# Differential attention, head by head: another order for VectorE's rotation products, combinations and output additions, and TensorE's next scores placed between sample products and value products

## The chip, the cores and the metric

The program runs on one core of a Trainium2 chip. The metric is the device time of one execution in microseconds. Three runs of the kernel before took 3537.03, 3538.32 and 3538.99 us (median 3538.32). The profile shows one execution of its own, which took 3538.83 us around a span of 3537.0 us from the first to the last instruction.

## The reference, cut to what matters

The reference is one step of a two-layer decoder over 1024 prompt tokens and 8 sample tokens (each of the 8 has 256 past positions in a paged cache). Layer 0 is a Mamba-2 mixer and an MLP. Layer 1 is differential attention with 8 heads, and an MLP. The change lies in the attention alone, which for one head computes

```python
sc = jnp.einsum('bqhmd,bkhmd->bhmqk', qi, k) * scale     # m = 0, 1: two score maps of width 64
sc = jnp.where(kpos[None, :] <= qpos[:, None], sc, -jnp.inf)
p = jax.nn.softmax(sc, axis=-1)
w = p[:, :, 0] - lam * p[:, :, 1]                         # the combination
o = jnp.einsum('bhqk,bkhe->bqhe', w, v)                   # values of width 128
o = rms_norm(o, subln_g) * (1.0 - lam_init)
out += o @ w_o[rows of this head]
# q and k come from projections of x, rotated: x1*cos - x2*sin, x2*cos + x1*sin
```

The eight sample tokens do the same against their past keys and values and their own new ones.

## The kernel before

The activations stand transposed in SBUF, 128 features by 1032 tokens a tile. The weights come as a stream of units of 128x1024 numbers. For each unit GpSimd makes a high and a low part (`split`, L321: the high part is L326, the low part L329), and a product is three matmuls: high by high, high by low, low by high. GpSimd starts on a unit when its load is there and when TensorE has begun the unit that frees the slot (`unit_begun`).

The attention stage works head by head. Each engine has its own hand-written order of the work of head n, a function `attend` (TensorE L724, ScalarE L1140, VectorE L1668), and runs its instructions strictly in that order; semaphores tie the engines together. Head 0 is written out, heads 1 to 6 are a loop, head 7 is written out. In head n three kinds of work are woven together:

- The queries of head n are taken in eight blocks, step i = 0 to 7, of growing width 128(i+1). TensorE computes both score maps into four PSUM banks (`scores`, L596, with the causal mask added by two small matmuls, L613). VectorE takes the row maxima (`maxima`, L1581), ScalarE the exponentials with their sums (`scores_exp`, L1060). VectorE weights and subtracts (`combine`, L1588: a reciprocal, a 128x1 operation L1593, a wide operation L1595, then `w_ready`). TensorE transposes the result (`turn`, L616), ScalarE copies it (`turned`, L1072), TensorE multiplies by the values (`values`, L630), ScalarE takes the result out (`output`, L1078). `scores(i)` may start when the exponentials of step i-1 have been taken (`p_ready`).
- The sample tokens: `sample_rows`, `sample_weights` and `sample_values` on TensorE (L695 to L720), and on VectorE `sample_max` (a copy out of PSUM, L1617, and a maximum, L1619), `sample_shares`, `sample_spread` (L1627) and `sample_out` (L1634). Together with `values` they share one PSUM bank, whose turns are counted by `m_free`.
- What belongs to the neighbouring heads. If `ahead`, TensorE projects queries, keys and values of head n+1 (`fill`, L638, three chunks for each; the matmuls are L647), and VectorE rotates them: two products over 128x1032 (`rope_products`, L1570) and their sum. If `fin`, head n-1 is normalized and multiplied by its rows of the output weights (`out_jobs`, L681: j = 0 to 7, three chunks each, into three banks; matmuls L690). VectorE adds every chunk to the residual (`add_outputs`, L1656), which frees its bank (`u_free`). Two of these three banks are also banks of the scores, so `scores(4)` waits for all 24 additions.

The line numbers are those of the profile.

Of the kernel before, what the change touches and what calls it, by code (L numbers as in the profile page):

```python
# [94 lines left out]
def half_of(m):  # L95

    return slice(HD * m, HD * m + HD)
# [23 lines left out]
def program(nc, a, o):  # L121
    with ExitStack() as ctx:
# [76 lines left out]
        rawq = sb("rawq", [P, T], F32, m)  # L199
        rawk = sb("rawk", [P, T], F32, m)  # L200
        rawv = sb("rawv", [P, T], F32, m)
        swq = sb("swq", [P, T], F32, m)
# [140 lines left out]
        def _(pe):  # L343
# [252 lines left out]
            def scores(n, i, fin):  # L596

                rows = slice(i * 128, (i + 1) * 128)
                width = (i + 1) * 128
                if i:  # L600
                    pe.wait_ge(s["p_ready"], 16 * n + 2 * i)
                elif fin:
                    pe.wait_ge(s["p_ready"], 16 * n)
                if i == 4 and fin:
                    pe.wait_ge(s["u_free"], 24 * n)
                diag = (width - 1) // 512
                for c0 in range(0, width, 512):
                    w = min(512, width - c0)
                    for m_ in range(2):
                        mm(aux[:, 2 * m_ + c0 // 512, 0:w], qr[half_of(m_), rows], kr[half_of(m_), c0:c0 + w],  # L610
                           start=True, stop=(c0 // 512 != diag))
                for m_ in range(2):
                    mm(aux[:, 2 * m_ + diag, width - 128 - 512 * diag:width - 512 * diag], mbf[:, 0], mbf[:, 1],  # L613
                       start=False, stop=True).then_inc(s["s_full"], 1)
# [15 lines left out]
            def values(h, i, n, use):  # L630

                pe.wait_ge(s["wt_ready"], 8 * h + i + 1)
                m_bank(n, use)
                for k in range(i + 1):
                    last = mm(aux[:, 4, 0:128], wt[:, k], vt[:, k], start=(k == 0), stop=(k == i))
                last.then_inc(s["o_full"], 1)
# [58 lines left out]
            def sample_rows(n):  # L695

                pe.wait_ge(s["ssc_ready"], n + 1)
                m_bank(n, 4)
                mm(aux[0:16, 4, 256:257], qkn[:].rearrange("p m b -> p (m b)"), one[:], start=True, stop=True)
                for g in range(PAGES):  # L700
                    last = nc.tensor.transpose(aux[0:16, 4, g * 128:(g + 1) * 128],
                                               ssc[:, g].rearrange("p m b -> p (m b)"), ident[:])
                last.then_inc(s["srow_full"], 1)

            def sample_weights(n):

                pe.wait_ge(s["sp_ready"], n + 1)
                m_bank(n, 7)
                for g in range(PAGES):
                    mm(aux[:, 4, g * 8:g * 8 + 8], srow[0:16, g * 128:(g + 1) * 128], pair[0:16, 0:8], start=True, stop=True)  # L710
                mm(aux[0:NB, 4, 16:17], pair[0:16, 0:8], srow[0:16, 256:257], start=True, stop=True).then_inc(s["wsm_full"], 1)

            def sample_values(n):

                pe.wait_ge(s["wsm_ready"], n + 1)
                pe.wait_ge(s["pv_in"], 16 * n + 16)
                m_bank(n, 9)
                for b in range(NB):
                    for g in range(PAGES):
                        last = mm(aux[0:NB, 4, 0:P], wpad[:, g, b], past[:, b * PAGES + g],  # L720
                                  start=(b == 0 and g == 0), stop=(b == NB - 1 and g == PAGES - 1))
                last.then_inc(s["so_full"], 1)

            def attend(at, n, fin, ahead):  # L724
                p = n - 1

                pe.wait_ge(s["rope_done"], 2 * n + 2)
                scores(n, 0, fin)
                queries(n, fin)
                if ahead:  # L730
                    q_slot = unit(at)
                    fill(q_slot, n, 0, 0)
                if fin:
                    values(p, 7, n, 1)
                turn_values(n)
                scores(n, 1, fin)
                turn(n, 0)
                if ahead:
                    fill(q_slot, n, 0, 1)
                pe.wait_ge(s["vt_ready"], n + 1)  # L740
                if fin:
                    turn_outputs(p)
                values(n, 0, n, 2)
                scores(n, 2, fin)
                turn(n, 1)
                if ahead:
                    fill(q_slot, n, 0, 2)
                if fin:
                    o_slot = unit(at)
                    out_jobs(o_slot, p, range(0, 4))  # L750
                values(n, 1, n, 3)
                scores(n, 3, fin)
                turn(n, 2)
                if fin:
                    out_jobs(o_slot, p, range(4, 8))
                sample_rows(n)
                values(n, 2, n, 5)
                scores(n, 4, fin)
                turn(n, 3)
                if ahead:  # L760
                    k_slot = unit(at)
                    fill(k_slot, n, 1, 0)
                values(n, 3, n, 6)
                scores(n, 5, fin)
                turn(n, 4)
                if ahead:
                    fill(k_slot, n, 1, 1)
                sample_weights(n)
                values(n, 4, n, 8)
                scores(n, 6, fin)  # L770
                turn(n, 5)
                if ahead:
                    fill(k_slot, n, 1, 2)
                sample_values(n)
                values(n, 5, n, 10)
                scores(n, 7, fin)
                turn(n, 6)
                if ahead:
                    v_slot = unit(at)
                    fill(v_slot, n, 2, 0)  # L780
                values(n, 6, n, 11)
                if ahead:
                    fill(v_slot, n, 2, 1)
                turn(n, 7)
                if ahead:
                    fill(v_slot, n, 2, 2)
# [449 lines left out]
        def _(dve):  # L1236
# [330 lines left out]
            stt(pair[:, 10:11], pair[:, 9:10], lam[0:16, 2:3], pair[:, 8:9], ALU.mult, ALU.add)  # L1567
            drain()

            def rope_products(h, raw, sw, swapped):  # L1570

                dve.wait_ge(s[swapped], 64 * h + 64)
                tt(raw[:], raw[:], cos[:], ALU.mult)
                tt(sw[:], sw[:], sin[:], ALU.mult)
                drain()

            def rope_sum(dst, raw, sw):
                tt(dst[:], raw[:], sw[:], ALU.add)
# [42 lines left out]
            def sample_shares(n):  # L1621
                dve.wait_ge(s["sexp_ready"], n + 1)
                nc.vector.reciprocal(st[0:16, 7:8], st[0:16, 7:8])
                drain()
                ts(srow[:, 0:257], srow[:, 0:257], st[0:16, 7:8], pair[:, 10:11], ALU.mult, ALU.mult).then_inc(s["sp_ready"], 1)
# [42 lines left out]
            def attend(n, fin, ahead):  # L1668
                p = n - 1
                maxima(n, 0)  # L1670
                sample_scores(n)
                combine(n, 0)
                if fin:
                    variance(p)
                maxima(n, 1)
                if fin:
                    normalize(p)
                combine(n, 1)
                maxima(n, 2)
                if fin:  # L1680
                    low_outputs(p)
                combine(n, 2)
                if fin:
                    add_outputs(p, range(0, 4))
                maxima(n, 3)
                if fin:
                    add_outputs(p, range(4, 6))
                combine(n, 3)
                if fin:
                    add_outputs(p, range(6, 8))  # L1690
                sample_max(n)
                maxima(n, 4)
                if ahead:
                    rope_products(n + 1, rawq, swq, "q_swap")
                combine(n, 4)
                sample_shares(n)
                maxima(n, 5)
                combine(n, 5)
                sample_spread(n)
                maxima(n, 6)  # L1700
                combine(n, 6)
                sample_out(n)
                maxima(n, 7)
                if ahead:
                    rope_sum(qr, rawq, swq)
                combine(n, 7)
                tt(e9[:], s1[:], s1[:], ALU.mult)
                drain()
                if ahead:
                    rope_products(n + 1, rawk, swk, "k_swap")  # L1710
                    dve.wait_ge(s["k_out"], 16 * n + 16)
                    rope_sum(kr, rawk, swk)
# [191 lines left out]
```

## Time and profile before

| | |
|---|---|
| median of three runs | 3538.32 us |
| the profiled execution / its span | 3538.83 / 3537.0 us |
| busy: TensorE matmul, weight load | 3310.9 us (94%), 3119.8 us (88%) |
| busy: VectorE, ScalarE, GpSimd | 2055.0 (58%), 952.5 (27%), 1007.8 us (28%) |
| mean granted clock of TensorE | 0.958 |
| attention, all heads | about 2036 to 2724 us of the span |

Busy time is the time in which an engine had an instruction at work. PE is TensorE, PEld its weight loads, DVE VectorE, ACT ScalarE, POOL GpSimd; a q behind the name is that engine's sequencer. The granted clock is a share of full speed: 1.00 is 2.4 GHz and 0.50 is 1.2 GHz. Matmuls overlap, so a row can end after the next has started.

### The profile page before, as it was taken

The numbers are of one execution on the slowest core, as the hardware profiler recorded it, in microseconds if no ns is written. First come the engines' busy times: TensorE is split into PE (matmuls) and PEld (weight loads), VectorE is DVE, ScalarE is ACT, GpSimd is POOL, SyncE is SP. The second block draws the span as 40 slices with busy tenths as digits, with TensorE's granted clock in tenths as the row PEclk, the third lists the DMA queues.
The fourth block names the chain that finished last, engine by engine and source line by source line (L and its number), as shares of the span: only waits on it lengthen the run. The fifth ranks groups of instructions, "written<-read, shape, count | busy, mean of one in ns | idle before, by whom it ended". The sixth has DMA issues, their size and how long they took to land.

```text
span 3537.0 us, 54842 instructions
## 1 busy us (share of the span) xinstructions
PE 3310.9 (94%) x20874; PEld 3119.8 (88%) x20874; DVE 2055.0 (58%) x3125; ACT 952.5 (27%) x2420; POOL 1007.8 (28%) x455
## 2 busy tenths in 40 slices
PE   7999999999998799999999889999986999999997
PEld 7889888888887799999999878888874999999997
DVE  7577677676676763343344756666665743333436
ACT  4334334343343221111110234333332311111112
POOL 3222232222221133333333222222210333333331
PEclk9899999999999699999999899999997899999997
DMA  3111111111111012431111222222210111111111
GB/s 109 45 49 45 49 51 45 37 63 45 43 52 43 19 42 83 140 109 46 48 48 47 66 82 84 71 82 73 71 60 6 37 48 43 48 49 48 44 47 54
DMA packets 86339, 200.86 MB, mean 57 GB/s; under 512 B 9416, under 2 KB 47176, under 8 KB 85616
## 3 DMA queue, kind: packets, MB, share of 16 engines
q1 hardware_dynamic: 35552, 139.54, 11.5%
q10 hardware_dynamic: 50592, 58.37, 5.4%
q8 instruction: 165, 2.70, 0.3%
q14 instruction: 30, 0.25, 0.0%
HBM read 166.86 MB, written 39.60 MB: 58 GB/s over the span
## 4 chain that ended last, share of the span: by engine, by line
issue 62%; PE 20%; POOLq 9%; POOL 6%; SPq 1%; DMA 1%; DVE 0%; ACT 0%; ACTq 0%; DVEq 0%
PE jb L353 20%; POOLq L328 9%; POOL wl L329 6%; SPq L301 1%; DMA wraw<-in_wstream 1%; PE aux L527 0%; ACT acc L1001 0%; DVE acc L1465 0%; POOLq L336 0%; POOLq L325 0%; SPq L278 0%; SPq L284 0%; DVE lnq L1469 0%; ACT lnq L989 0%; PE aux L534 0%
## 5 line engine op out<-in xcount | busy, mean ns | idle before, releaser
L326 POOL TENSOR_TENSOR wh<-wraw,one 128x1024 fp32r<-128x1024 f32 x225 | 439.5, 1954 | 2432.1 <-PE jb L353 1690.5
L353 PE MATMUL jb<-xh,wh 128*128 128x344 f32 x2616 | 846.8, 324 | 24.5 <-issue 12.3
L353 PE MATMUL jb<-xl,wh 128*128 128x344 f32 x2616 | 838.2, 320 | 0.0
L353 PE MATMUL jb<-xh,wl 128*128 128x344 f32 x2616 | 837.8, 320 | 0.0
L329 POOL TENSOR_TENSOR wl<-wraw,wh 128x1024 fp32r<-128x1024 f32 x225 | 568.0, 2524 | 32.0
L1281 DVE TENSOR_TENSOR acc<-jb,acc 128x344 f32<-128x344 f32 x504 | 255.6, 515 | 460.4 <-PE jb L353 455.9
L353 PEld LDWEIGHTS jb<-xh,wh 128*128 128x128 f32 x2616 | 494.1, 189 | 31.4 <-issue 20.0
L353 PEld LDWEIGHTS jb<-xl,wh 128*128 128x128 f32 x2616 | 494.0, 189 | 0.1
L353 PEld LDWEIGHTS jb<-xh,wl 128*128 128x128 f32 x2616 | 493.9, 189 | 0.0
L353 PE MATMUL jb<-hh,wh 128*128 128x344 f32 x1536 | 492.3, 320 | 0.0
L353 PE MATMUL jb<-hl,wh 128*128 128x344 f32 x1536 | 490.9, 320 | 0.0
L353 PE MATMUL jb<-hh,wl 128*128 128x344 f32 x1536 | 490.4, 319 | 0.0
L1035 ACT ACTIVATE rl<-jb 128x344 f32<-128x344 f32 x192 | 87.9, 458 | 1064.1 <-PE jb L353 1037.1
L1522 DVE TENSOR_TENSOR rl<-rl 128x344 f32<-128x344 f32 x192 | 158.3, 825 | 363.3 <-ACT hh L1037 363.2
L353 PEld LDWEIGHTS jb<-hh,wh 128*128 128x128 f32 x1536 | 288.8, 188 | 3.4 <-DVE acc L1281 3.4
L353 PEld LDWEIGHTS jb<-hh,wl 128*128 128x128 f32 x1536 | 288.5, 188 | 0.0
L353 PEld LDWEIGHTS jb<-hl,wh 128*128 128x128 f32 x1536 | 288.1, 188 | 0.0
L1524 DVE TENSOR_TENSOR hl<-rl,hh 128x344 fp32r<-128x344 f32 x192 | 228.9, 1192 | 14.3
L1317 DVE SCALAR_TENSOR_TENSOR ct<-pre,pg,ct 128x344 f32<-128x344 f32 (+1 forms) x288 | 201.3, 701 | 42.7 <-ACT ct L896 23.9
L1586 DVE TENSOR_REDUCE st<-aux 128x1 f32<-128x256 f32 (+7 forms) x128 | 90.9, 751 | 138.5 <-PE aux L613 138.4
L647 PE MATMUL jb<-xh,wh 128*128 128x344 f32 x504 | 166.4, 330 | 0.0
L647 PE MATMUL jb<-xh,wl 128*128 128x344 f32 x504 | 161.1, 320 | 0.0
(263 smaller groups left out, 5190.8 us busy)
## 6 DMA issues: line engine op xcount, KB each, us to landing
wraw<-in_wstream SPq DMA_DIRECT2D x225, 512.0 KB, 3.2
pre<-in_state ACTq DMA_DIRECT2D x16, 512.0 KB, 4.3
out_ssm_s<-pre ACTq DMA_DIRECT2D x16, 512.0 KB, 3.2
kgat<-in_cache_k SPq DMA_DIRECT2D x16, 512.0 KB, 5.2
vgat<-in_cache_v SPq DMA_DIRECT2D x16, 512.0 KB, 6.3
past<-kgat ACTq DMA_DIRECT2D x8, 1024.0 KB, 5.7
past<-vgat ACTq DMA_DIRECT2D x8, 1024.0 KB, 5.7
acc<-in_xT SPq DMA_DIRECT2D x8, 516.0 KB, 7.0
```

Of the source, the lines that this page charges most:

```text
L301: pages = [sp.value_load(a["ptab"][0:1, k:k + 1], min_val=0, max_val=PHYS - 1) for k in range(NB * PAGES)]
L326: nc.gpsimd.tensor_tensor(wh[slot][:].rearrange("p k m -> p (k m)"), wraw[:, slot].rearrange("p k m -> p (k m)"), one[:].to_broadcast([P, ...
L328: pool.drain()
L329: nc.gpsimd.tensor_tensor(wl[slot][:], wraw[:, slot], wh[slot][:].bitcast(F32), ALU.subtract).then_inc(w_split, 1)
L353: last = mm(jb[:, c, 0:CW], w[slot][:, j * kt + k], x[:, k, cols], start=(k == 0 and p == 0), stop=(k == kt - 1 and p == 2))
L647: last = mm(jb[:, 2, 0:CW], w[slot][:, k], x[:, k, c * CW:(c + 1) * CW], start=(k == 0 and p == 0), stop=(k == KD - 1 and p == 2))
L1035: af(rl[:, x % 4], jb[:, x % 3, 0:CW], ACT.Relu).then_inc(bank_free[x % 3], 1)
L1281: tt(acc[:, k, cols], jb[:, c, 0:CW], acc[:, k, cols], ALU.add).then_inc(bank_free[c], 1)
L1317: last = stt(ct[:, t0:t1], src[:, 1 + k + t0:1 + k + t1], w(k), ct[:, t0:t1], ALU.mult, ALU.add)
L1522: tt(rl[:, x % 4], rl[:, x % 4], rl[:, x % 4], ALU.mult)
L1524: tt(hl[b][:, j, cols], rl[:, x % 4], f(hh[b][:, j, cols]), ALU.subtract).then_inc(s["h_ready"], 1)
L1586: nc.vector.tensor_reduce(st[:, m_:m_ + 1], src, AX.X, ALU.max, negate=True).then_inc(s["nmax_ready"], 1)
```

## The change

VectorE: the additions of the output jobs 4 to 7 of the head before now stand together ahead of `combine(3)`; before, `combine(3)` stood between those of job 5 and job 6. The two rotation products of the next queries, which stood together between `maxima(4)` and `combine(4)`, are taken apart: the product with the cosine comes behind `sample_shares`, ahead of `maxima(5)`, and the product with the sine behind `combine(5)`, ahead of `sample_spread`. The rotation of the keys is as before.

TensorE: in three places `values` and the following `scores` change places. The scores of step 4 now come right behind `sample_rows`, those of step 6 behind `sample_weights`, those of step 7 behind `sample_values`. ScalarE's order, GpSimd's and the DMA queues' are not touched, and no instruction is added or removed.

```diff
@@ TensorE, attend
                 sample_rows(n)
+                scores(n, 4, fin)
                 values(n, 2, n, 5)
-                scores(n, 4, fin)
                 turn(n, 3)
...
                 sample_weights(n)
+                scores(n, 6, fin)
                 values(n, 4, n, 8)
-                scores(n, 6, fin)
                 turn(n, 5)
...
                 sample_values(n)
+                scores(n, 7, fin)
                 values(n, 5, n, 10)
-                scores(n, 7, fin)
                 turn(n, 6)
@@ VectorE
-            def rope_products(h, raw, sw, swapped):
+            def rope_cos(h, raw, swapped):
 
                 dve.wait_ge(s[swapped], 64 * h + 64)
                 tt(raw[:], raw[:], cos[:], ALU.mult)
+
+            def rope_sin(sw):
                 tt(sw[:], sw[:], sin[:], ALU.mult)
                 drain()
+
+            def rope_products(h, raw, sw, swapped):
+                rope_cos(h, raw, swapped)
+                rope_sin(sw)
@@ VectorE, attend
                 maxima(n, 3)
                 if fin:
-                    add_outputs(p, range(4, 6))
+                    add_outputs(p, range(4, 8))
                 combine(n, 3)
-                if fin:
-                    add_outputs(p, range(6, 8))
                 sample_max(n)
                 maxima(n, 4)
-                if ahead:
-                    rope_products(n + 1, rawq, swq, "q_swap")
                 combine(n, 4)
                 sample_shares(n)
+                if ahead:
+                    rope_cos(n + 1, rawq, "q_swap")
                 maxima(n, 5)
                 combine(n, 5)
+                if ahead:
+                    rope_sin(swq)
                 sample_spread(n)
```

## Rows read from the trace of the kernel before

**Rows 1.** Loop marks on VectorE; stretches: busy us (instructions) by engine, PEclk, DMA, GB/s.
```profile
L1572 DVEq FUSED_REGOPS  x6: 46/46/53, 2149.9 to 2565.1; - x6
...
2315.80:2398.90 83.10, 79.02 (x540) 69.30 (x538) 54.62 (x91) 31.19 (x86) 18.69 (x8) 1.00 0.25 76
...
2648.00:2700.00 52.00, 34.06 (x185) 25.09 (x186) 18.99 (x34) 18.50 (x48) 0.00 (x0) 0.78 0.00 0
...
2820.00:2860.00 40.00, 40.00 (x255) 39.76 (x254) 22.33 (x24) 8.55 (x18) 15.72 (x8) 1.00 0.16 53
```

**Rows 2.** TensorE's waits, 2149.7 to 2647: total us, times, longest.
```profile
PE jb L620 <- DVEq L1596: 10.3, 6, 1.7
PE jb L690 <- DVE acc L1661: 7.6, 7, 1.1
PE aux L635 <- DVE os L1636: 2.6, 6, 0.4
PE aux L635 <- DVE srow L1617: 2.5, 5, 0.5
...
PE aux L635 <- DVE wpad L1630: 2.0, 6, 0.3
```

**Rows 3.** Timeline around job 7 and step 4, one looped head: start, us, engine, [idle before].
```profile
2392.30 0.75 DVE L1595 SCALAR_TENSOR_TENSOR pp<-pp,st 128x512 f32<-128x512 f32 x1
...
2393.82 0.42 PE L690 MATMUL jb<-ah,wh 128*128 128x344 f32 x1 [1.09 <-DVE acc L1661]
...
2395.99 0.41 DVE L1617 COPY srow<-aux 16x257 f32<-16x257 f32 x1
2396.46 0.94 PE L635 MATMUL aux<-vt,wt 128*128 128x128 f32 x6 [0.51 <-DVE srow L1617]
...
2397.32 1.35 PE L610 MATMUL aux<-kr,qr 64*128 64x512 f32 x8
...
2399.09 0.40 PE L647 MATMUL jb<-xh,wh 128*128 128x344 f32 x1
```

**Rows 4.** Timeline from the first key projection to turn(4), same head.
```profile
2316.06 0.40 PE L647 MATMUL jb<-xh,wh 128*128 128x344 f32 x1
...
2316.54 1.89 POOL L326 TENSOR_TENSOR wh<-wraw,one 128x1024 fp32r<-128x1024 f32 x1 [14.43 <-PE jb L647]
...
2319.45 3.38 DVE L1574 TENSOR_TENSOR swq<-swq,sin 128x1032 f32<-128x1032 f32 x1
...
2322.40 0.29 PE L613 MATMUL aux<-mbf 128*128 128x128 bf16 x2
...
2323.44 0.88 DVE L1595 SCALAR_TENSOR_TENSOR pp<-pp,st 128x640 f32<-128x640 f32 x1
...
2324.41 0.77 PE L620 MATMUL jb<-ident,pp 128*128 128x128 f32 x5 [1.72 <-DVEq L1596]
```

**Rows 5.** Timeline: GpSimd's low parts, a 128x1 operation, a key product.
```profile
2348.48 3.16 POOL L329 TENSOR_TENSOR wl<-wraw,wh 128x1024 fp32r<-128x1024 f32 x1
...
2349.79 1.87 DVE L1593 SCALAR_TENSOR_TENSOR st<-s,st,lam 128x1 f32<-128x1 f32 x1
...
2353.39 1.23 DVE L1573 TENSOR_TENSOR rawk<-rawk,cos 128x1032 f32<-128x1032 f32 x1
...
2382.75 2.40 POOL L329 TENSOR_TENSOR wl<-wraw,wh 128x1024 fp32r<-128x1024 f32 x1
```

**Rows 6.** Timeline of head 0 (first two) and of head 7.
```profile
2062.41 1.62 PE L635 MATMUL aux<-vt,wt 128*128 128x128 f32 x6 [2.65 <-DVE srow L1617]
...
2063.96 2.51 PE L610 MATMUL aux<-kr,qr 64*128 64x512 f32 x8
...
2664.28 2.48 PE L635 MATMUL aux<-vt,wt 128*128 128x128 f32 x10 [3.31 <-DVE wpad L1630]
...
2671.48 1.01 ACT L1069 ACTIVATE pp<-aux,st 128x896 f32<-128x896 f32 x1 [4.16 <-DVE st L1586]
...
2684.07 2.19 PE L635 MATMUL aux<-vt,wt 128*128 128x128 f32 x9 [3.69 <-ACT wt L1075]
```

## The prediction, made before the changed kernel ran

> **What bounds the kernel now.** I read the page first (busy shares and the 40 slices), then the stretches of the attention stage, then who waited for whom on TensorE, then the timeline of one head. The page says TensorE is busy 94% of the span; so a change pays only where TensorE stands idle or runs at its low clock. The change touches only the attention stage, so the stretches come next. The loop's register instruction on VectorE starts six times between 2149.9 and 2565.1, which makes one head (2565.1 - 2149.9) / 5 = 83.04 us long; in such a head TensorE is busy 79.0, VectorE 54.6, ScalarE 31.2, GpSimd 18.7 us, and the granted clock is 1.00 [rows 1]. About 4.1 us of each head is TensorE waiting, and the reader should see that nothing but VectorE ends those waits. Over the six looped heads [rows 2]: 1.7 us each for the combined weights of step 4 (turn(4) waits for combine(4)'s `w_ready`), 1.1 each for output additions, 0.5 for the copy of the sample row, 0.3 for the spread sample weights, 0.4 for sample_out. VectorE is idle for a third of the head, so these are waits for its order, not for its capacity. Head 7 has nothing to fill with and its last 52 us run at a mean clock of 0.78 [rows 1].
>
> I name the stops of a head A (output additions), B (sample-row copy), C (turn(4)), D (spread), E (sample_out). All durations are from the profiled execution: 3538.83 us around a span of 3537.0; the median of the runs shown is 3538.32, 0.5 less.
>
> **A and B: additions together, combine(3) after them, scores(4) before values(2).** Before, combine(3) with its 0.75 us product at 2392.30 stands between the additions of j=5 and j=6; TensorE's output job 7 needs the first addition of j=6, and waits 1.09 us until 2393.82. The copy of the sample row runs at 2395.99 to 2396.40, values(2) starts at 2396.46, scores(4) at 2397.32, the next projection at 2399.09 [rows 3]. After: job 7 follows job 6. That saves the 1.09, some 0.15 by which back-to-back groups overlap, and some 0.2 that job 7 lost between its chunks: 1.45. The two last additions end about 0.5 us after TensorE's last output job, as before. scores(4) needs all additions (its banks are the ones they read), so it starts about 0.2 us after sample_rows, and takes 1.35 plus its masks, 1.6 in all. Beneath it VectorE does combine(3) (0.16 + 0.22 + 0.75 with drains, 1.3) and then the copy (0.41), 1.8 in all: values(2) waits about 0.3 us for the copy. So B keeps its 0.5 in two pieces; A goes. **1.4 us a head, heads 1 to 7: 9.9.** combine(3) itself ends 3.3 us later than now, and turn(3) behind values(2) finds it 1.4 us old. The maxima of step 4 wait behind the row's maximum (0.4) but still come 0.6 us earlier against the projection than now. In head 0 there are no additions; values(2) waits 2.65 us for the copy, and the scores(4) that follow take 2.51 at the low clock [rows 6]. They can now start about when combine(3) does, some 1.1 us after sample_rows, and cover most of that wait: **1.5 us**, once.
>
> **C: cosine product behind combine(4), sine product behind combine(5).** I count from F, the start of the first key projection (2316.06). GpSimd's split starts at F+0.5 (1.89 us, then the low parts). Both rotation products read two SBUF operands and lie on this split: the sine product takes 3.38 us, until 2322.83; combine(4) comes behind it (0.88 at 2323.44); TensorE is done with scores(5) at 2322.69 and starts turn(4) at 2324.41 [rows 4]. Clear of GpSimd a product takes 1.23 [rows 5]. Nothing shown has combine(4) on the split, so I bound it. The nearest row is combine(7), whose 128x1 operation, 0.22 elsewhere, takes 1.87 and ends with GpSimd's low-part operation (2348.48 + 3.16 = 2351.64) [rows 5]. The inputs of combine(4) are there at about F+2.1. Lower bound: it is not held up, w_ready at F+3.6. Upper bound: held until the low parts end, which are 2.40 undisturbed and 3.16 when disturbed [rows 5], so until F+4.9 to F+5.7, plus 0.88 and a drain: F+5.9 to F+6.7. TensorE wants it at F+6.5, once the masks of scores(5) are out. I take the upper row's F+5.9 (the operation is the same one): hidden, with 0.6 to spare, and 0.2 us exposed at the far end. So C goes: **1.72 + 0.15 overlap = 1.9 us.** What is late next: sample_shares ends near F+6.7, the cosine product (1.23, GpSimd is done) F+7.8; the maxima of step 5 start there instead of F+8.9. exp(5) (two passes of 0.9 behind the first maximum) ends near F+10.7, combine(5) F+12.3, and scores(6), now straight behind the sample weights at F+11.6, finds it ready.
>
> The Trainium skill ("SBUF — State Buffer", section "SBUF: two separate sides") says that VectorE with two SBUF inputs and a reading GpSimd exclude one another for a whole instruction, whichever starts first. The two long products and combine(7) bear this out. It speaks against the move, since combine(4) now stands on the split instead of a rotation product; by that rule it ends near F+5.9, by a shared bandwidth near F+4, and neither is later than TensorE.
>
> **D and E.** The sine product (1.23) now stands ahead of sample_spread: spread ends near F+13.9. TensorE has scores(6) (1.8 us and masks) until F+13.7, so values(4) still waits about 0.3: **D gains nothing.** If the sine product were 3.38 there, D would be 2.5 us; no unit begins in that stretch, so GpSimd has nothing to do. E: scores(7) (2.3 us with masks) covers the 0.34 us of sample_out; the 0.43 (2.6 in six waits) [rows 2] goes. I count **0.2 us** for D and E together, since the spread comes some 0.2 late by the drain behind the sine product. The other edge of the new placement is ScalarE, whose order is not changed: exp(7) stands behind output(5), and that now behind scores(7). Counting from the end of sample_values: scores 2.3, values(5) to 3.8, output(5) to 4.4, exp(7) to 6.7, turned(6) to 7.6, and TensorE wants it at 8.3, behind its projection. It costs nothing, with 0.7 us to spare. The query sum moves with the maxima of step 7 to the edge of GpSimd's next split, where it now lies partly; the key rotation after it has over 3 us to spare.
>
> C to E: 1.9 + 0.2 = 2.1 us, heads 0 to 6: **14.7.**
>
> **Head 7.** No rotation and no projection: here a chain of scores, maxima, exp, transposes decides. values(4) waits 3.31 us for the spread weights at 2664.28, scores(6) come behind, exp(6) at 2671.48, values(6) waits 3.69 at 2684.07 [rows 6]. Now scores(6) can start at once behind the sample weights, because exp(5) is done 1.2 us later; they fill the 3.31. exp(6) then waits for output(4), and ends some 2.5 us sooner counted with A's gain taken out. scores(7) gain the 1.13 us before values(5) too. By that chain values(6) comes 3.6 us sooner; if scores(7) fall at the low clock (twice 2.0 us), 1.9. I take **3.3.**
>
> **Sum.** 9.9 + 1.5 + 14.7 + 3.3 = 29.4 us; looped head 83.04 - 3.5 = 79.5 us. 3538.8 - 29.4 = 3509.4; for a median, 0.5 less: **3509 us.** The clock takes none of it back as far as rows show: a stretch of the last layers with TensorE busy 40.00 of 40 us is at 1.00 [rows 1].
>
> **Rivals.**
> Half of it comes back. combine(4) meets the split twice (small operation behind the high parts, its product behind disturbed low parts) and is late by up to 1 us, the copy in B comes 0.5 later, D grows by 0.5: 7 x 2 = 14 us less, 3522. For: each of these margins is under 1 us. Against: all are measured durations, and the loop repeats to 0.1 us.
> Only TensorE's placement acts: VectorE remains late for turn(4), because something not seen orders it. Then A (9.9) and head 7 remain, with 1.5: 3524. Against: combine(4)'s only inputs are the two exponentials.
> Slower: the low clock enters the loop. Heads 0 and 7 show clocks under 1.00 around waits of 2.65 to 3.7 us, the loop with at most 1.7 none [rows 1, 2, 6]. If a new wait of 2.65 or more arose in each head, for instance output(5) before exp(7) holding values(6), or sine against a split before the spread, the 4.0 us projection behind it would take 8: 6.7 us a head against 3.5 gained, seven heads, +22 us, 3560. It decides from a wait of about 2.5 us; the largest I find is 0.3.
> The Trainium skill ("TensorE: Matmul & The Clock Gate", section "HAM oscillation — how this bites in real kernels") has such idle gaps bring the low clock back, over and over; the loop's clock of 1.00 says its gaps don't, and they get shorter.
> No change: the chain shifts to another engine. VectorE at 54.6 of 83 us and nothing else near leaves little room.
>
> **Chances.** Forecast (3500 to 3516) 0.67; half comes back 0.18; placement only 0.06; no change 0.04; slower 0.05. 0.2% is 7 us, about what a measurement tells from no change. Faster by more 0.91, within 0.04, slower 0.05. Range 3501 to 3523: from one us more in each head to the first rival.
>
> **What would show it.** After: the looped heads at 79.5 us; turn(4) no longer waiting; job 7 of the outputs without wait; a wait of 0.1 to 0.3 before scores(4) for additions and 0.3 before values(2); values(4) still 0.3 behind the spread; no wait for sample_out; rotation products near 1.23, one small operation of combine(4) near 2 us. Wrong: waits for the combine of step 3, 4 or 5, values(6) waiting for ScalarE, or a clock under 1.00 in heads 1 to 6.

## The result

The changed kernel takes 3493.23 us (median of four runs, 3489.76 to 3495.83) against 3537.73 us for the kernel before (four runs): a ratio of 0.9871, 95% interval 0.9859 to 0.9884, 44.5 us faster. The prediction had the direction, but gave 3509 us and a range of 3501 to 3523; the time lies 8 us outside it, on the fast side.

### The profile page after: what moved, and what is told of

Same layout as the page of the kernel before. It is cut to its first block, busy times and chain, and to the rows that moved or that the text cites. A ratio compares the mean times of both kernels' runs of the same rounds, so it can differ in the third digit from the quotient of the medians.

```text
span 3494.0 us, 54842 instructions
## 1 busy us (share of the span) xinstructions
PE 3298.9 (94%) x20874; PEld 3116.5 (89%) x20874; DVE 2047.4 (59%) x3125; ACT 951.5 (27%) x2420; POOL 1003.6 (29%) x455
## 4 chain that ended last, share of the span: by engine, by line
issue 61%; PE 21%; POOLq 10%; POOL 6%; SPq 1%; DMA 0%; DVE 0%; ACT 0%; ACTq 0%; DVEq 0%
PE jb L353 20%; POOLq L328 9%; POOL wl L329 6%; SPq L301 1%; DMA wraw<-in_wstream 0%; PE aux L527 0%; ACT acc L1001 0%; DVE acc L1465 0%; POOLq L336 0%; POOLq L325 0%; SPq L278 0%; SPq L284 0%; DVE lnq L1469 0%; ACT lnq L989 0%; PE aux L534 0%
## 5 line engine op out<-in xcount | busy, mean ns | idle before, releaser
L353 PE MATMUL jb<-xl,wh 128*128 128x344 f32 x2616 | 838.5, 321 | 0.0
L329 POOL TENSOR_TENSOR wl<-wraw,wh 128x1024 fp32r<-128x1024 f32 x225 | 557.5, 2478 | 32.0
L647 PE MATMUL jb<-xl,wh 128*128 128x344 f32 x504 | 160.9, 319 | 0.0
```

What stands on the lines that cost most here:

```text
L329: nc.gpsimd.tensor_tensor(wl[slot][:], wraw[:, slot], wh[slot][:].bitcast(F32), ALU.subtract).then_inc(w_split, 1)
L353: last = mm(jb[:, c, 0:CW], w[slot][:, j * kt + k], x[:, k, cols], start=(k == 0 and p == 0), stop=(k == kt - 1 and p == 2))
L647: last = mm(jb[:, 2, 0:CW], w[slot][:, k], x[:, k, c * CW:(c + 1) * CW], start=(k == 0 and p == 0), stop=(k == KD - 1 and p == 2))
```

## Time and profile after

| span of the profiled executions | before | after | saved | forecast |
|---|---|---|---|---|
| head 0 | 75.07 us | 70.75 | 4.3 | 3.6 |
| each of heads 1 to 6 | 83.03 | 78.42 | 4.62 | 3.5 |
| head 7 with its end | 113.77 | 101.90 | 11.9 | 4.7 |
| whole span | 3537.0 | 3494.0 | 43.0 | 29.4 |

A head is counted from TensorE's first query broadcast (L660) to that of the next head; head 7 to the first sum of the layer norm (L521). The stages before and behind lost 0.9 us together.

The loop marks and two stretches after, against [rows 1]; the columns are those of [rows 1]. The first mark is now on the loop of (2542.6 - 2150.5) / 5 = 78.42 us. The second line is a looped head, the third head 7.

```profile
L1572 DVEq FUSED_REGOPS  x6: 46/46/53, 2150.5 to 2542.6; - x6
...
2342.88:2421.30 78.42, 78.08 (x538) 69.23 (x537) 53.85 (x90) 31.18 (x87) 18.03 (x8) 1.00 0.26 80
2578.15:2680.05 101.90, 74.67 (x413) 57.03 (x411) 67.18 (x132) 30.52 (x86) 8.96 (x4) 0.87 0.10 32
```

The same stretch of head 7 in the kernel before:

```profile
2609.77:2723.54 113.77, 82.18 (x413) 62.31 (x411) 67.54 (x132) 30.66 (x86) 8.94 (x4) 0.80 0.09 28
```

In the loop TensorE is busy 78.08 of 78.42 us: little is left there for an order to gain. In head 7 its *busy time* fell by 7.5 us though it has the same matmuls, and the clock rose from 0.80 to 0.87.

TensorE's waits over much the same stretch, with the start of head 7, against [rows 2] (total, times, longest):

```profile
PE aux L610 <- DVE acc L1667: 1.0, 6, 0.3
PE aux L635 <- DVE srow L1623: 0.9, 6, 0.2
PE jb L620 <- DVEq L1602: 0.7, 1, 0.7
```

The waits for the combination, for output job 7 and for sample_out are gone (the 0.7 is one in head 7), and of that for the spread some 0.2 us is left, which this table doesn't show for the matmuls. What stays besides are the two small waits of B, 0.16 us each. The timeline of one looped head shows them, against [rows 3]:

```profile
2376.97 1.35 PE L610 MATMUL aux<-kr,qr 64*128 64x512 f32 x8 [0.16 <-DVE acc L1667]
...
2377.35 0.75 DVE L1601 SCALAR_TENSOR_TENSOR pp<-pp,st 128x512 f32<-128x512 f32 x1
...
2378.22 0.41 DVE L1623 COPY srow<-aux 16x257 f32<-16x257 f32 x1
...
2378.69 0.94 PE L635 MATMUL aux<-vt,wt 128*128 128x128 f32 x6 [0.16 <-DVE srow L1623]
...
2379.82 0.41 PE L647 MATMUL jb<-xh,wh 128*128 128x344 f32 x1
```

combine(3) and the copy run beneath scores(4). And the stretch of C, against [rows 4] and [rows 5]; F is 2379.82:

```profile
2380.30 1.89 POOL L326 TENSOR_TENSOR wh<-wraw,one 128x1024 fp32r<-128x1024 f32 x1 [12.95 <-PE jb L647]
...
2382.34 2.38 POOL L329 TENSOR_TENSOR wl<-wraw,wh 128x1024 fp32r<-128x1024 f32 x1
2382.40 3.00 DVE L1601 SCALAR_TENSOR_TENSOR pp<-pp,st 128x640 f32<-128x640 f32 x1
...
2386.08 1.21 DVE L1573 TENSOR_TENSOR rawq<-rawq,cos 128x1032 f32<-128x1032 f32 x1
2386.27 0.71 PE L620 MATMUL jb<-ident,pp 128*128 128x128 f32 x5
...
2391.77 1.23 DVE L1576 TENSOR_TENSOR swq<-swq,sin 128x1032 f32<-128x1032 f32 x1
...
2393.05 0.28 PE L613 MATMUL aux<-mbf 128*128 128x128 bf16 x2
...
2393.15 0.16 DVE L1636 COPY wpad<-aux 128x16 f32<-128x16 f32 x1
...
2393.37 1.19 PEld L635 LDWEIGHTS aux<-vt,wt 128*128 128x128 f32 x10 [0.20 <-DVE wpad L1636]
2393.37 1.38 PE L635 MATMUL aux<-vt,wt 128*128 128x128 f32 x10
```

combine(4) now meets GpSimd's split, though not with the operation that was forecast: its 128x1 operation takes 0.22 us as elsewhere, and its wide operation takes 3.00 us instead of 0.88. It ends at F+5.6 (forecast F+5.9), 0.9 before TensorE starts turn(4). The rotation products run clear of the split. The matmuls of values(4) show no wait, but the weight load ahead of them waits 0.20 us for the spread, and values(4) starts 0.32 us after the masks (L613) do. In the run rot_back below, where the spread is done long before, this is 0.12. So some 0.2 us of D's wait is left.

Head 7, against [rows 6]:

```profile
2618.51 1.16 PE L635 MATMUL aux<-vt,wt 128*128 128x128 f32 x8 [2.24 <-ACT wt L1075]
...
2625.44 1.77 PE L610 MATMUL aux<-kr,qr 64*128 64x512 f32 x8 [1.28 <-ACT pp L1069]
...
2627.48 1.35 PE L635 MATMUL aux<-vt,wt 128*128 128x128 f32 x10
...
2640.69 3.36 PE L635 MATMUL aux<-vt,wt 128*128 128x128 f32 x14 [3.20 <-ACT wt L1075]
```

values(4) waits no more and takes 1.35 us where it took 2.48: it runs at the high clock now. values(6) still waits 3.2 and then runs at the low one.

## The experiments

All are against the kernel before in the same job (its medians there: 3538.0 to 3538.8). "Head" is a looped head.

**1. Each engine's part alone.** VectorE's part without TensorE's, and the reverse:

```diff
 # v_only: the changed kernel, TensorE's attend as before
-                scores(n, 4, fin)
                 values(n, 2, n, 5)
+                scores(n, 4, fin)
... (likewise for scores 6 and 7)
 # t_only: the kernel before, with only TensorE's three exchanges
```

> VectorE's part alone (additions together, rotation products apart), TensorE's order as before. Theory 1 (the two parts need each other: each VectorE move puts work in front of what values waits for, and only the scores in front of values cover it): values(2) waits for a copy that comes behind combine(3), so the 1.36 us of the output additions turn into about 2 us of wait for the sample row; values(4) waits about 2 us for the spread behind the sine product; turn(4) waits no more. Looped head 82.5 to 83 us (before 83.03, after 78.41), head 7 within 2 us of before (113.8), in all 0 to 6 us faster than before. Rival (the parts add up, VectorE's order is what TensorE waited for): looped head near 83.0 - 1.4 - 1.9 = 79.7, some 25 us faster.

> TensorE's part alone (scores before values in three places), VectorE's order as before. Theory 1: the wait for output additions (1.1) and the one for turn(4) (1.5 to 1.7) stay, the waits before values(4) and values(5) go: looped head 81.0 to 81.7 us, head 7 about 104 to 106 us (its gain is TensorE's order), in all 17 to 22 us faster. Rival (the parts add up): what is missing from 44.5 us beyond VectorE's 25, so 20 us, with a looped head near 81.7 too; the two are told apart by the sum with the other part alone: about 22 us by theory 1, 44 by the rival.

| | time, us | ratio (95%) | head | head 7 |
|---|---|---|---|---|
| v_only | 3554.81 | 1.0044 (1.0027 to 1.0060) | 83.0 to 87.4 | 114.3 |
| t_only | 3513.17 | 0.9930 (0.9913 to 0.9947) | 81.1 | 104.1 |

VectorE's part alone is 16 us *slower* than nothing (forecast 0 to 6 faster); the other gives 25 us (forecast 17 to 22, which left out the 4.4 us of head 0); together 44.5 instead of 9. The rival of a plain sum is out. v_only's waits over its six looped heads, and one of these heads:

```profile
PE aux L635 <- DVE srow L1623: 11.3, 6, 1.9
PE aux L635 <- DVE wpad L1636: 9.9, 6, 2.2
PE aux L635 <- DVE os L1642: 2.6, 6, 0.4
...
2280.18:2366.01 85.83, 81.60 (x538) 71.26 (x537) 53.60 (x90) 31.28 (x87) 17.90 (x8) 0.96 0.25 74
```

The wait for turn(4) and the one for the additions are gone, but values(2) waits 1.9 us for the copy behind combine(3), and values(4) 1.2 to 2.2 for the spread behind the sine product. The waits were forecast; that heads reach 87.4 us was not. The granted clock goes with it: one of the six heads has the waits of 1.88 and 2.2 us at a clock of 1.00 and takes 83.0 us, as forecast; the five others are at 0.94 to 0.96 and take 85.2 to 87.4. In those five the scores(4) right behind the wait of 1.88 take 1.84 to 2.51 us instead of 1.35. This is the prediction's slower rival, here and not in the whole change.

**2. The whole change in head 7 only, and everywhere but there.**

```diff
 # head7_new: each of the edits only `if not ahead`; head7_old: only `if ahead`
+                if not ahead:
+                    scores(n, 6, fin)
+                    values(n, 4, n, 8)
+                else:
+                    values(n, 4, n, 8)
+                    scores(n, 6, fin)
```

> The whole change in head 7 only (where there are no rotation products); heads 0 to 6 in the order of before. Theory A (head 7 gains 11.9 us by its own order: less waiting, and so a higher clock behind it): head 7 falls from 113.8 to about 102 us, looped heads stay at 83.03, in all 12 us faster. Theory B (part of it is the phase in which TensorE's clock meets the start of head 7): the first output jobs, before any edit of head 7, take 10.8 us as before instead of 8.5, head 7 gains 9.9 or less, in all 6 to 10 us faster.

> The whole change in heads 0 to 6, head 7 in the order of before. Theory A: looped heads 78.41 us, head 0 70.75, head 7 at 113.8: 32 us faster than before. Theory B: head 7's first output jobs take 8.5 us as in the changed kernel, head 7 about 111.8 or less, 34 us or more faster than before.

| | time, us | ratio (95%) | head | head 7 |
|---|---|---|---|---|
| head7_new | 3529.24 | 0.9975 (0.9966 to 0.9985) | 83.04 | 101.8 |
| head7_old | 3503.98 | 0.9901 (0.9885 to 0.9918) | 78.41 | 111.8 |

Neither theory fits both. Head 7's order alone gives 12.0 us of that head in the profile, as theory A had it, but 9.4 in the medians, and the old order behind the new heads is 2.0 us shorter than before, as theory B had it. The first output jobs, ahead of every edit of head 7, took 10.8 us before, 8.5 in head7_new and 9.9 in head7_old. The changed kernel itself has 8.5 in its first profile and 10.6 in its second (after_again, below). So these 2 us differ from one execution to the next and are not shown to be an effect of either half.

**3. One part taken back at a time.** Each is the changed kernel but for:

```diff
 # rot_back: both rotation products between maxima(4) and combine(4) again
 # adds_back: combine(3) between the additions of jobs 5 and 6 again
 # s4_back: values(2) ahead of scores(4) again
 # s67_back: values(4) ahead of scores(6), values(5) ahead of scores(7) again
 # s67_rot_back: s67_back and rot_back together
```

> The changed kernel with both rotation products back between maxima(4) and combine(4). Theory: the wait before turn(4) comes back (1.6 to 1.8 us) and nothing else: looped head 80.1 to 80.5 us against 78.41, clock 1.00 in the loop, head 7 (no rotation) 101.9 within 2, in all 12 to 15 us slower than the changed kernel. Rival (scores(4) before values(2) already starts maxima(4) early enough, so that the products run ahead of GpSimd's split): looped head under 79.2.

> The changed kernel with combine(3) back between the output additions of job 5 and job 6. Theory: output job 7 waits 1.1 us again, the sample row's copy comes straight behind the additions and no longer counts: looped head 79.4 to 79.7 us against 78.41, head 7 about 1.3 longer, in all 8 to 10 us slower than the changed kernel. Rival (the grouping only moves the wait on to scores(4), which wait for all additions anyway): looped head under 78.8.

> The changed kernel with values(2) back ahead of scores(4). Theory: values(2) waits 1.9 us for the copy behind combine(3), as with VectorE's part alone. If the clock holds, the looped head is 79.8 to 80.1 us and the clock 1.00; if one wait of 1.9 us is enough to bring the low clock (as seen with VectorE's part alone), heads differ, from 79.9 to 82, with a clock of 0.96 to 0.98. In all 11 to 25 us slower than the changed kernel. Rival (scores(4) in front is worth only its 0.5 us of before): looped head 78.9.

> The changed kernel with values(4) back ahead of scores(6), and values(5) ahead of scores(7). Theory: values(4) waits about 2 us for the spread behind the sine product, values(5) 0.4: looped head 80.7 to 81.1 us with the clock at 1.00, more (up to 83) where the low clock enters; head 7 some 6 us longer, in all 20 to 32 us slower than the changed kernel. Rival (these two places are worth the 0.3 and 0.4 us that they waited before, as the prediction had it): looped head near 79.1, in all 8 us slower.

> The changed kernel with the rotation products back between maxima(4) and combine(4), and values(4) and values(5) back ahead of scores(6) and scores(7): of the change only the grouped additions and scores(4) ahead of values(2) are left. Theory (the wait before values(4) with those scores behind it comes from the sine product ahead of the spread): values(4) waits 0.3, values(5) 0.4 again, the clock stays at 1.00, looped head 79.0 to 79.4 us; head 7, which has no rotation, as in s67_back (112.4, within 4); in all 24 to 30 us faster than before. Rival (the places themselves): looped head 81 us or more.

| | time, us | ratio (95%) | head | head 7 |
|---|---|---|---|---|
| rot_back | 3497.52 | 0.9882 (0.9865 to 0.9898) | 78.17 | 105.9 |
| adds_back | 3504.16 | 0.9905 (0.9889 to 0.9922) | 79.42 | 106.1 |
| s4_back | 3515.99 | 0.9938 (0.9921 to 0.9954) | 81.3 to 81.8 | 106.6 |
| s67_back | 3534.19 | 0.9992 (0.9982 to 1.0001) | 82.7 to 84.3 | 112.4 |
| s67_rot_back | 3525.24 | 0.9962 (0.9948 to 0.9976) | 80.6 to 82.2 | 110.1 |

adds_back came as forecast: the additions' wait is worth 1.0 us a head. rot_back did not: with the products in their *old* place a head is 0.24 us shorter than in the changed kernel, and turn(4) waits for nothing. (The whole kernel is not shown to be faster: 3497.52 us against 3493.23 and, measured again, 3495.26; head 7 took 105.9 in this profile.) First rot_back, then t_only, whose only difference from it is that the additions are split:

```profile
2377.12 1.53 DVE L1592 TENSOR_REDUCE st<-aux 128x1 f32<-128x640 f32 x2
...
2377.88 0.40 PE L647 MATMUL jb<-xh,wh 128*128 128x344 f32 x1
...
2378.36 4.34 POOL L326 TENSOR_TENSOR wh<-wraw,one 128x1024 fp32r<-128x1024 f32 x1 [12.94 <-PE jb L647]
...
2378.59 1.21 DVE L1573 TENSOR_TENSOR rawq<-rawq,cos 128x1032 f32<-128x1032 f32 x1
...
2379.73 1.21 DVE L1576 TENSOR_TENSOR swq<-swq,sin 128x1032 f32<-128x1032 f32 x1
...
2384.33 0.72 PE L620 MATMUL jb<-ident,pp 128*128 128x128 f32 x5
```

```profile
2384.80 1.56 DVE L1592 TENSOR_REDUCE st<-aux 128x1 f32<-128x640 f32 x2 [0.76 <-PE aux L613]
...
2385.74 0.40 PE L647 MATMUL jb<-xh,wh 128*128 128x344 f32 x1
...
2386.22 1.89 POOL L326 TENSOR_TENSOR wh<-wraw,one 128x1024 fp32r<-128x1024 f32 x1 [13.95 <-PE jb L647]
2386.28 2.93 DVE L1573 TENSOR_TENSOR rawq<-rawq,cos 128x1032 f32<-128x1032 f32 x1
...
2389.13 3.39 DVE L1576 TENSOR_TENSOR swq<-swq,sin 128x1032 f32<-128x1032 f32 x1
...
2394.09 0.76 PE L620 MATMUL jb<-ident,pp 128*128 128x128 f32 x5 [1.74 <-DVEq L1602]
```

In rot_back the two products take 1.21 us each and it is GpSimd that waits: its operation takes 4.34 us, and no wait of TensorE comes of it. In t_only the products take 2.93 and 3.39, and turn(4) waits 1.74. Earlier maxima are not the reason. Counted from F (2377.88 and 2385.74), the maxima of step 4 (L1592) end at F+0.77 in rot_back and F+0.62 in t_only, the cosine product is recorded from F+0.71 and F+0.54, and GpSimd's operation from F+0.48 in both. The product comes *earlier* in the run in which it waits. What makes the difference is open.

The four runs with TensorE's new order show what VectorE's two moves are worth, one looped head each:

| | products together, old place | products apart |
|---|---|---|
| additions split | 81.12 (t_only) | 79.42 (adds_back) |
| additions together | 78.17 (rot_back) | 78.42 (the changed kernel) |

turn(4) waits in t_only alone. So either move takes C's wait away: grouping the additions gives 2.95 us, A and C together, and taking the products apart on top of it costs 0.24.

s4_back (as forecast) and s67_back (39 to 41 us slower than the changed kernel where 20 to 32 was forecast, and with that not shown to be faster than the kernel before) show what the places of the scores are worth with VectorE's new order: 3 and 5 us a head, not the 0.5 and 0.7 that was waited there before. The part of s67_rot_back was missed too: I expected heads of 79.0 to 79.4 us and 24 to 30 us in all, and it gives 13.5. values(4) waits 1.3 us even without the sine product: TensorE arrives there at F+11.6, where it arrived at F+13.5 before, and the spread is done only at F+12.9. The low clock comes again in five of the six heads. One looped head of each of s4_back and s67_back, then two of s67_rot_back, the one at 1.00 and one of the others:

```profile
2272.53:2354.32 81.79, 79.59 (x538) 70.03 (x537) 53.97 (x90) 31.20 (x87) 18.04 (x8) 0.98 0.26 77
```

```profile
2272.76:2355.61 82.85, 80.16 (x538) 70.19 (x537) 53.65 (x90) 31.17 (x87) 17.91 (x8) 0.98 0.26 76
```

```profile
2188.29:2268.88 80.59, 78.52 (x538) 69.23 (x537) 54.30 (x90) 31.08 (x87) 21.03 (x8) 1.00 0.27 78
2268.88:2351.11 82.23, 80.17 (x538) 69.75 (x537) 54.31 (x90) 31.08 (x87) 21.04 (x8) 0.98 0.26 77
```

The two heads of s67_rot_back have the same waits (1.3 and 0.4 us) and differ by 1.64 us, all of it TensorE's busy time: that is the low clock's part there. The rest of what the head lost is waits.

**4. Head 7: how much is the clock.** The same kernel again; idle matmuls that compute nothing put into TensorE's waits of head 7; ScalarE's copies ahead of exponentials there; and these together with rot_back.

```diff
 # fill7, in TensorE's attend and finish, nine places; fill7_half has half the numbers
+            def warm(k):
+                for _ in range(k):
+                    mm(jb[:, 2, 0:128], ident[:], ident[:], start=True, stop=True)
+                if not ahead:
+                    warm(22)
                 values(n, 6, n, 11)
 # act7, in ScalarE's attend, i = 4 to 7
+                if not ahead:
+                    turned(n, i - 1)
                 scores_exp(n, i)
+                if ahead:
+                    turned(n, i - 1)
 # both7: fill7, act7, rot_back;  best: fill7_half, act7, rot_back
```

> The changed kernel once more, for a second profile and as the base of the next three. If head 7's length hangs on where TensorE's clock stands when it begins, looped heads repeat at 78.41 us and head 7 may differ from 101.9 by up to some 4 us; if not, both repeat within 0.2.

> The changed kernel with idle matmuls (identity by identity into a free bank, 0.11 us each) in TensorE's waits of head 7, each group some 80% of the wait it stands in. They add work and compute nothing. Theory (of head 7's 101.9 us several are the low clock after waits): the clock of the head is 0.95 or more instead of 0.82, the first output jobs take 7.3 us instead of 8.5, scores(5) and turn(4) 2.3 instead of 3.8, values(6) 1.7 instead of 3.4; head 7 96 to 98.5 us. Rival (head 7 is held by the chain through VectorE and ScalarE, the clock is only a symptom): 101 us or longer.

> The changed kernel with ScalarE's turned(i-1) ahead of scores_exp(i) for steps 4 to 7 of head 7 alone. Theory (values(3) waits 2.2 and values(6) 3.2 us for a copy that stands behind two exponentials which need not come first): both waits shrink by 1.5 to 2.5 us, the chain by the part that TensorE does meanwhile; head 7 1.5 to 3.5 us shorter than in the changed kernel, looped heads 78.41. Rival (the exponentials are the chain and now come 0.6 to 0.9 us later each): head 7 the same or up to 3 us longer.

> The changed kernel with the rotation products back in their old place (which cost nothing in its loop: 78.17), the idle matmuls, and ScalarE's other order in head 7. Theory: looped heads 78.17, head 7 93 to 96.5 us, 6 to 10 us faster than the changed kernel, near 3485. Rival: the two edits of head 7 take from the same waits, so that together they give no more than the better one alone.

> The changed kernel with half as many idle matmuls in head 7 (0.235 us each: 40 to 90% of each wait). They compute nothing. Theory (the low clock costs head 7 several us): clock 0.95 or more, head 7 96 to 99 us. Rival (held by the chain): 101 us or longer even so.

> As fill7_half, with the rotation products in their old place and ScalarE's copies ahead of the exponentials in steps 4 to 7 of head 7. Theory: looped heads 78.17, head 7 94 to 98 us and the same in every execution, 5 to 9 us faster than the changed kernel. Rival: head 7 no shorter than fill7_half's, in all 2 us faster than it (the loop's 0.24 a head).

| | time, us (lowest to highest) | ratio (95%) | head | head 7 |
|---|---|---|---|---|
| after_again | 3495.26 (3494.45 to 3496.34) | 0.9881 (0.9865 to 0.9898) | 78.42 | 105.6 |
| fill7 | 3495.02 (3493.18 to 3496.12) | 0.9881 (0.9865 to 0.9898) | 78.42 | 102.5 |
| act7 | 3494.28 (3489.48 to 3497.49) | 0.9877 (0.9860 to 0.9893) | 78.42 | 101.3 |
| both7 | 3492.87 (3490.31 to 3496.44) | 0.9874 (0.9858 to 0.9891) | 78.17 | 104.1 |
| fill7_half | 3490.48 (3487.88 to 3491.53) | 0.9861 (0.9845 to 0.9878) | 78.42 | 98.1 |
| best | 3487.74 (3486.39 to 3488.28) | 0.9855 (0.9838 to 0.9871) | 78.17 | 95.9 |

Head 7 of after_again, fill7_half and best:

```profile
2573.74:2679.36 105.62, 77.71 (x414) 58.81 (x412) 67.79 (x132) 30.52 (x86) 8.96 (x4) 0.84 0.09 31
```

```profile
2578.28:2676.34 98.06, 81.41 (x532) 65.30 (x530) 68.12 (x132) 30.52 (x86) 8.95 (x4) 0.97 0.10 33
```

```profile
2576.53:2672.47 95.94, 80.28 (x532) 64.62 (x530) 68.03 (x132) 30.57 (x86) 8.96 (x4) 0.96 0.11 34
```

The same code takes 101.9 or 105.6 us for head 7, with the clock at 0.87 or 0.84, while the looped heads repeat to 0.02 us. (Head 0 came out at 68.4 and 70.8, so the spans differ by 0.8 only.) With the 59 idle matmuls (118 records in the profile) head 7 is 3.8 to 7.6 us faster in the profiles, one profile of fill7_half against the two of the changed kernel; the medians differ by 2.8 and 4.8 us, and its runs (3487.88 to 3491.53) overlap with the changed kernel's first four. fill7 was mis-sized by me: such a matmul takes some 0.23 us (two records) and not the 0.11 of a transpose, so its groups ran past the waits and gave back what the clock gained; both7 has the same fault. act7's waits shrank as forecast (values(3) 2.24 to 0.69, values(6) 3.20 to 1.01), yet the head is only 0.6 to 4.3 us shorter, which the 3.7 us between two executions of one kernel don't resolve. best is faster than the changed kernel: its slowest run is 1.5 us below that kernel's fastest of eight, its median 5.5 to 7.5 us below. Its three edits weren't timed apart beyond fill7_half; of its lead over that one (2.7 us), 1.5 are the loop's 0.25 in six heads.

## Why the prediction was wrong

The mechanism held in the main: TensorE waited for VectorE's order, and the change took nearly all of these waits away. Two terms of the sum were too small: head 7's, by 3.5 to 7.2 us, and that of C to E, by 7. (Head 0's own 1.5 came out at 1.2; the stages outside the attention lost 0.9.)

- **Head 7: forecast 4.7 us (1.4 of A and 3.3), measured 11.9, or 8.2 by the second profile.** The step that failed is "by that chain values(6) comes 3.6 us sooner": counted from `sample_rows`, behind A, it came 8.5 us sooner, or 6.8 by the second profile. The step moved the waits and kept each operation's duration, and even took low-clock durations as the cautious case. The idle time of TensorE in the head did shrink by about the forecast: 31.6 us before, 27.2 and 27.9 after, so 4.4 and 3.7 against 4.7. The rest, 7.5 and 4.5 us, is *busy time* of the same matmuls at a higher clock, a term that the sum put at nothing. scores(6) and values(4) took 3.36 and 2.48 us before and 1.77 and 1.35 after. fill7_half, which gives TensorE nothing but a higher clock (0.97), takes another 3.8 to 7.6 us off the head. The two profiles of one kernel, and head7_old's 2.0 us without any edit in the head, show that up to some 4 us of this can come from the execution and not from the change, which a range of 22 us should have named as a cause.
- **C to E: forecast 2.1 us a head, measured 3.1.** By projections: from the first key projection to the second 8.87 us before and 6.94 after (C 1.9, as forecast); to the third 8.72 and 8.41 (D 0.3, forecast nothing); to the value projection 12.31 and 11.66 (E 0.65, of which I wrote down 0.2); from there to the next head 14.71 and 14.48 (0.23, not in the sum). D failed on "spread ends near F+13.9": it ended at F+13.5, because combine(4) ended 0.3 earlier than its bound; some 0.2 of D's wait is left. E's 0.43 of wait had been cut to 0.2 for a drain ahead of the spread, while a group behind a wait also loses its overlap with the one ahead, as I had counted in A and C. The last 0.23 was a wait of values(6) too short for the table of waits. Times seven this is 7 us.
- **C's cause.** "C goes" has the right size, but the move that it was put down to is only one of two that do it. adds_back has the products apart and the additions split, and C goes; rot_back keeps the products where they were and groups the additions, and C goes as well. The prediction took grouping to act on A alone. It also had the wrong operation of combine(4) on the split (the 128x1 one for the wide one); the low parts end at F+4.9 for either, so combine(4) ended near its bound all the same. With the additions together, the products apart cost 0.24 us a head, for the spread behind the sine product.
- **A and B: 1.4 us a head, measured 1.49.** Both pieces of B's wait are where they were put (0.16 and 0.16 for 0.2 and 0.3). adds_back gives the split additions 1.00.
- **The rivals.** "Half comes back" and "placement only" did not happen. The slower rival's mechanism is real: v_only, s4_back, s67_back and s67_rot_back have it, with heads longer by 1.6 us in s67_rot_back and by 2.1 to 4.4 in v_only than the one head of each that is at 1.00. Its threshold of 2.5 us was wrong: in v_only the clock fell behind a wait of 1.88, in s67_rot_back behind one of 1.3, while the kernel before has 1.72 and 1.09 in each head at 1.00. Nor does the longest wait tell: that one head has waits as long as those of the others.

What stays open: why grouping the additions lets VectorE's products go ahead of GpSimd in rot_back, with records that start in the reverse order; what decides in which head the clock falls; and how much of act7's gain is real.

## What to carry to other kernels

Reorderings on two engines have to be judged together (here 16 us lost by one alone, 25 won by the other alone, 44.5 won together): an operation put ahead of what TensorE waits for costs nothing only if TensorE has independent work in front of that wait. Look at each engine's order as one pair. Where waits of 1 to 4 us lie close together on TensorE, price the matmuls behind them at both clocks, and do not reuse the durations of the old profile; filling such a wait with idle matmuls shorter than the wait is worth a try where no real work is left. Before believing a reason, put back the part that the reason names, and the other parts one by one: two moves may each do what one was made for.

## What was not expected of the hardware

- Two operands in SBUF against GpSimd: in rot_back GpSimd's operation is recorded from 2378.36, VectorE's product from 2378.59, and yet the product takes 1.21 us and GpSimd's operation 4.34, in every looped head. In t_only the records are 0.06 us apart in the same order and VectorE waits (2.93). The product that comes closer behind GpSimd is the one that waits. The Trainium skill ("SBUF — State Buffer", section "SBUF: two separate sides") has the first to start keep the port for its whole instruction; the durations agree with such a lock, the recorded starts do not say who holds it.
- The granted clock of a program on one core is not the same in two executions: 0.87 and 0.84 over head 7 of one kernel, 101.9 and 105.6 us.
- An idle 128x128 matmul of fp32 tiles took some 0.23 us at the high clock (two records, 0.112 us from start to start in most groups of fill7_half), a transpose of the same size 0.11 (one record).
